# Queries and keys of six latent heads in two parts with three score passes, and three centred tiles instead of four in the second norms

## The reference, cut to what matters

```python
# heads B: 8 heads, query and key of 96 rows (64 from the latent projection, 32 with rotary positions)
s = einsum("bhqd,bhkd->bhqk", q, k) * 96 ** -0.5
p = softmax(s); o = einsum("bhqk,bhkd->bhqd", p, v)
# after the mixer, and again after the feed-forward:
z = ALPHA * x + f(x)
x = (z - mean(z)) * rsqrt(var(z) + eps) * g + b
```

## Time and profile before

| | us |
|---|---|
| median of 3 runs | 2478.61 (2478.15 to 2480.41) |
| the profiled execution, its own time | 2479.52 |
| its span, first to last instruction | 2477.7 |
| PE busy, share of the span | 2409.3, 97% |
| POOL busy | 1895.6, 77% |
| DVE busy | 1168.4, 47% |
| ACT busy | 697.4, 28% |
| mean granted TensorE clock | 0.995 |

### The profile page before, as it was taken

How to read it: one execution, slowest core, us unless ns; L and a number is a source line. 1 busy time by engine, 2 the same in 40 slices (tenths; PEclk the granted TensorE clock), 3 DMA queues, 4 the chain that set the end, 5 groups by cost and what they waited for, 6 DMA issues and landing times.

```text
span 2477.7 us, 32293 instructions
## 1 busy us (share of the span) xinstructions
PE 2409.3 (97%) x11126; PEld 1861.6 (75%) x11126; DVE 1168.4 (47%) x1581; ACT 697.4 (28%) x1262; POOL 1895.6 (77%) x1543
## 2 busy tenths in 40 slices
PE   8999999999999999999999999999999999999998
PEld 6755778888778844788888777767888877678886
DVE  6576443333271477533342485655322656553223
ACT  2266242330021166232220233244010241440101
POOL 8712688889888743898888798836999888369995
PEclk9999999999999999999999999999999999999999
DMA  4201122222223200232222232211222232112222
GB/s 178 85 17 35 60 78 100 93 102 93 94 77 111 85 26 9 70 109 93 95 93 101 77 115 102 85 43 60 94 102 93 94 102 94 39 57 101 93 102 85
DMA packets 57548, 207.12 MB, mean 84 GB/s; under 512 B 6512, under 2 KB 6896, under 8 KB 57200
## 3 DMA queue, kind: packets, MB, share of 16 engines
q1 hardware_dynamic: 55872, 199.87, 23.2%
q10 hardware_dynamic: 1584, 5.96, 0.7%
HBM read 203.71 MB, written 2.10 MB: 83 GB/s over the span
## 4 chain that ended last, share of the span: by engine, by line
PE 85%; DVE 6%; POOL 5%; issue 2%; ACT 1%; DMA 1%; DVEq 0%; POOLq 0%; SPq 0%; ACTq 0%
PE bank L733 23%; PE bank L735 23%; PE bank L734 23%; PE bank L838 3%; PE bank L789 3%; POOL w_hi L2646 2%; POOL w_lo L2649 2%; PE bank L897 2%; PE bank L867 2%; PE bank L918 1%; DMA ring<-in_weights 1%; DVE branch_lo L1934 1%; DVE work L1974 1%; DVE work L1991 1%; PE bank L937 1%
## 5 line engine op out<-in xcount | busy, mean ns | idle before, releaser
L2646 POOL TENSOR_TENSOR w_hi<-ring,unit 128x512 fp32r<-128x512 f32 x734 | 826.6, 1126 | 439.2 <-PE bank L735 300.8
L2649 POOL TENSOR_TENSOR w_lo<-ring,w_hi 128x512 fp32r<-128x512 f32 x734 | 998.2, 1360 | 57.5
L733 PE MATMUL bank<-moving_hi,w_hi 128*128 128x512 f32 x1834 | 723.4, 394 | 21.9 <-DVE moving_lo L2233 9.9
L735 PE MATMUL bank<-moving_hi,w_lo 128*128 128x512 f32 x1834 | 715.8, 390 | 0.0
L734 PE MATMUL bank<-moving_lo,w_hi 128*128 128x512 f32 x1834 | 715.6, 390 | 0.0
L733 PEld LDWEIGHTS bank<-moving_hi,w_hi 128*128 128x128 f32 x1834 | 345.3, 188 | 106.7 <-issue 20.6
L734 PEld LDWEIGHTS bank<-moving_lo,w_hi 128*128 128x128 f32 x1834 | 345.6, 188 | 72.8 <-issue 1.9
L735 PEld LDWEIGHTS bank<-moving_hi,w_lo 128*128 128x128 f32 x1834 | 345.0, 188 | 72.9
L2593 DVE TENSOR_TENSOR region<-region,bank 128x512 f32<-128x512 f32 x64 | 39.7, 681 | 278.4 <-PE bank L735 278.4
L1871 ACT ACTIVATE region<-bank 128x512 f32<-128x512 f32 x64 | 38.1, 598 | 363.5 <-PE bank L735 363.4
L733 PE MATMUL bank<-hid_hi,w_hi 128*128 (+1 forms) x352 | 137.7, 391 | 0.0
(11 more groups left out here) (334 smaller groups left out, 3603.8 us busy)
## 6 DMA issues: line engine op xcount, KB each, us to landing
ring<-in_weights SPq DMA_DIRECT2D x375, 512.0 KB, 3.2
x<-in_x_t ACTq DMA_DIRECT2D x4, 512.0 KB, 8.4
out<-region SPq DMA_DIRECT2D x8, 256.0 KB, 2.2
region<-in_tables ACTq DMA_DIRECT2D x1, 1312.0 KB, 6.2
region<-in_tables ACTq DMA_DIRECT2D x1, 1024.0 KB, 5.7
region<-in_p_t ACTq DMA_DIRECT2D x2, 512.0 KB, 5.3
region<-in_tables SPq DMA_DIRECT2D x1, 320.0 KB, 10.3
small_w<-in_small_w ACTq DMA_DIRECT2D x1, 320.0 KB, 6.0
```

The lines of the kernel that those rows point to most:

```text
L733: pe.matmul(bank, lhs[0], rhs[0], start=start, stop=False, skip_group_check=True)
L735: return pe.matmul(bank, lhs[1], rhs[0], start=False, stop=stop, skip_group_check=True)
L2646: pool.tensor_tensor(w_parts[0][:, s, at], ring[:, s, at], unit[:, 0:1].broadcast_to([P, BLK // 2]), ALU.mult).then_inc(split_hi, 1)
L2649: pool.tensor_tensor(w_parts[1][:, s, at], ring[:, s, at], w_parts[0][:, s, at].bitcast(F32), ALU.subtract).then_inc(split_ready, 1)
```

## The change

Three things. First, POOL makes two fp32r parts of the queries and keys of heads B2 to B7 (units B1 to B3), in a new `split_heads`, called ahead of the split of ("mixout", 0, 0): for each of 3 units, 2 tensors and 2 heads, one multiplication by 1 and one subtraction over 96 partitions x 512, so 24 operations. The lower part is written over the whole tile. `scores` waits for a unit's four splits at its first turn and makes three fp32r passes for each head in place of the one f32 matmul. Unit B0 stays as it was. Secondly, `CENTRED` goes from (1, 4, 1, 4) to (1, 3, 1, 3): in the second norms DVE centres three tiles, POOL five. Thirdly, POOL does four of these (tiles 3 to 6) where it did four before (tiles 4 to 7), and the last one (tile 7) between the two halves of its split of ("plegate", layer, 1).

```diff
-CENTRED = (1, 4, 1, 4)
+CENTRED = (1, 3, 1, 3)
...
+        ab_lower = [nc.alloc_sbuf_tensor_at(f"{name}_b_lo", [P, 8, S], F32R, offset=region_at + 1024 * kb)
+                    for name, kb in (("q", 64), ("k", 92))]
+        ab_upper = [nc.alloc_sbuf_tensor_at(f"upper_b_{n}", [P, S], F32R, offset=region_at + 1024 * kb)
+                    for n, kb in enumerate((88, 90, 108, 110, 112, 114, 116, 118, 120, 122, 124, 126))]
...
-                for c in range(2):
-                    mm = pe.matmul(at[c], q(u, c)[:, i * P:i * P + P], k(u, c)[:, 0:w], start=True, stop=True)
+                if in_parts and in_parts(u, i):
+                    for a, b in ((0, 0), (0, 1), (1, 0)):
+                        for c in range(2):
+                            q_part, k_part = in_parts(u, i)[c]
+                            mm = pe.matmul(at[c], q_part[a][:, i * P:i * P + P], k_part[b][:, 0:w], start=(a + b == 0),
+                                           stop=(a == 1), skip_group_check=True)
+                else:
+                    for c in range(2):
+                        mm = pe.matmul(at[c], q(u, c)[:, i * P:i * P + P], k(u, c)[:, 0:w], start=True, stop=True)
...
+                def parts_b(u, i):
+
+                    j = u[1]
+                    if u[0] == "A" or j == 0:
+                        return None
+                    if i == 0:
+                        pe.wait_ge(heads_split, 4 * j)
+                    rows = slice(0, B_QK)
+                    return [[(ab_upper[4 * (j - 1) + 2 * part + c][rows, :], ab_lower[part][rows, 2 * j + c, :])
+                             for part in range(2)] for c in range(2)]
...
-                early, ahead = (2, 3) if i % 2 else (0, 1)
+                early, ahead = (2, CENTRED[i]) if i % 2 else (0, CENTRED[i])
...
-                    if ahead <= n < CENTRED[i]:
-                        centre(n)
-                        dve.wait_ge(centered, sum(CENTRED[:i]) + n + 1)
...
-            def split(s, n, used=None):
+            def split(s, n, used=None, between=None):
...
+                    if h and between:
+                        between()
...
+            def split_heads():
+
+                pool.wait_ge(roped, ROPE_AT[("qB", 1)] + 1)
+                pool.wait_ge(qb_stored, B_HEADS)
+                rows, n = slice(0, B_QK), 0
+                for j in range(1, B_HEADS // 2):
+                    for part, whole in enumerate((q_b, k_b)):
+                        if j == 1 and part:
+                            pool.wait_ge(kb_stored, B_HEADS)
+                            pool.wait_ge(kpe_spread, B_HEADS // 2)
+                        for c in range(2):
+                            hi, lo = ab_upper[n][rows, :], ab_lower[part][rows, 2 * j + c, :]
+                            tile = whole[rows, 2 * j + c, :]
+                            n += 1
+                            pool.tensor_tensor(hi, tile, unit[rows, 0:1].broadcast_to([B_QK, S]), ALU.mult).then_inc(head_upper, 1)
+                            pool.wait_ge(head_upper, n)
+                            pool.tensor_tensor(lo, tile, hi.bitcast(F32), ALU.subtract).then_inc(heads_split, 1)
...
-            def recentre(i):
+            def recentre(i, last=KD):
...
-                for n in range(CENTRED[i], KD):
+                for n in range(KD - 1 if last is None else CENTRED[i], last or KD):
...
+            def recentre_odd(i):
+
+                recentre(i, KD - 1)
+                n = AT[("plegate", i // 2, 1)]
+                split(n % RING, n, (16 * (n // RING) + 16, n - RING + 1), lambda: recentre(i, None))
+
...
-            for key, between in ((("gate", 0, 0), lambda: recentre(0)), (("pleproj", 0, 0), lambda: recentre(1)),
+            for key, between in ((("mixout", 0, 0), split_heads), (("gate", 0, 0), lambda: recentre(0)), (("pleproj", 0, 0), lambda: recentre_odd(1)),
...
-                ahead = 1 if key[0] == "mixout" else RING
+                ahead = key[1] if key[0] == "mixout" else RING
```

More of the change, by code:

```diff
@@ L582, in build @@
         scored, maxed, exped, scaled = sem("scored"), sem("maxed"), sem("exped"), sem("scaled")
+        head_upper, heads_split = sem("head_upper"), sem("heads_split")
         turned, pt_stored, weighed, attended = sem("turned"), sem("pt_stored"), sem("weighed"), sem("attended")
@@ L828, in tokens_values, with scores @@
                     mm.then_inc(block_done, 1)
-            def scores(u, i, q, k, extra, causal=False):
+            def scores(u, i, q, k, extra, causal=False, in_parts=None):
                 t = TURN_AT[(u, i)]
@@ L845, in heads_in_pairs @@
             def heads_in_pairs(units, q, k, v, extra, causal=False, seed=None, between=None, last_rope=None,
-                               second=None, opened=None):
+                               second=None, opened=None, in_parts=None):
                 turns = [(u, i) for u in units for i in range(ST)]
@@ L879, in heads_in_pairs @@
                         second()
-                    scores(u, i, q, k, extra, causal)
+                    scores(u, i, q, k, extra, causal, in_parts)
                     if last_rope and i == 0:
@@ L889, in heads_in_pairs @@
                     if n + AHEAD < len(turns):
-                        scores(*turns[n + AHEAD], q, k, extra, causal)
+                        scores(*turns[n + AHEAD], q, k, extra, causal, in_parts)
                     t = TURN_AT[(u, i)]
@@ L1180, in last_keys @@
                         pe.wait_ge(roped, ROPE_AT[("qkA", 7)] + 1)
+                def parts_b(u, i):
[7 more added lines that the diff above has]
+                             for part in range(2)] for c in range(2)]
                 heads_in_pairs([u for u in UNITS if u[0] == kind], q, k, v, lambda u: [],
-                               last_rope=("qkA", 6) if kind == "A" else None, opened=opened,
+                               last_rope=("qkA", 6) if kind == "A" else None, opened=opened, in_parts=parts_b,
                                between=last_keys if kind == "A" else None)
@@ L2694, in _ @@
                 split(s, s)
+            def recentre_odd(i):
+                recentre(i, KD - 1)
+                n = AT[("plegate", i // 2, 1)]
+                split(n % RING, n, (16 * (n // RING) + 16, n - RING + 1), lambda: recentre(i, None))
             at = RING
-            for key, between in ((("gate", 0, 0), lambda: recentre(0)), (("pleproj", 0, 0), lambda: recentre(1)),
+            for key, between in ((("mixout", 0, 0), split_heads), (("gate", 0, 0), lambda: recentre(0)), (("pleproj", 0, 0), lambda: recentre_odd(1)),
                                  (("mixout", 1, 0), lambda: scale_first([u for u in UNITS if u[0] == "C"])),
-                                 (("gate", 1, 0), lambda: recentre(2)), (("pleproj", 1, 0), lambda: recentre(3))):
-                ahead = 1 if key[0] == "mixout" else RING
+                                 (("gate", 1, 0), lambda: recentre(2)), (("pleproj", 1, 0), lambda: recentre_odd(3))):
+                ahead = key[1] if key[0] == "mixout" else RING
                 split_up_to(at, AT[key] + ahead)
@@ L2702, in _ @@
                 between()
+                if key[0] == "pleproj":
+                    at += 1
             for layer in range(DEPTH):
```

## The result

| | before | after |
|---|---|---|
| median of 9 runs of each, us | 2479.48 | 2486.37 |
| lowest and highest, us | 2478.15 to 2481.80 | 2483.30 to 2488.84 |
| span of the profiled execution, us | 2477.7 | 2485.0 |

The ratio is 1.0025, with a 95% interval of 1.0017 to 1.0033: the change makes the kernel slower by 4 to 8 us. The forecast was 2487.3 in a range of 2474 to 2492.

A forecast was written before the change was run, and what follows sets the result against it. PE, busy 97% of the span, was taken as the bound, with DVE setting turns 1 to 3 of heads B. Heads +11.7 and norms -3.0 made +8.7 us, from 2478.6 to about 2487.3, range 2474 to 2492.

The forecast's parts named there:

- POOL's work on DVE: Heads B, turns 1 to 3: four DVE operations wait for POOL, 3.7 us a turn; turn 5 13.7 us late.
- that sign: Heads B, changed profile: the chain of waits should go through DVE and POOL from 203 to 237 us.
- The copy beside POOL: Heads B: DVE's copy from SBUF waits 0.97 us for a POOL operation, taken between nothing and 0.97.
- Scores on PE: Heads B: six fp32r matmuls take 1.57 us against 1.82, 0.25 us less a turn, 2.0 over eight turns.
- PE's clock in heads B: Heads B, PE's gaps of about 3 us in three turns: half rate costs nothing, up to 3 us for the range.
- The rival that priced this at up to 3 us: Heads B: PE at 1.2 GHz behind the gaps costs up to 3 us more, 2488 to 2491 us; chance 0.12.
- Norms: Second norms: 1.8 us gained in layer 0 and 1.2 in layer 1, 3.0 together, bounds 1.0 and 4.7.
- The start: Second norms: PE starts the pair of gate blocks 1.95 us earlier, at POOL's split instead of DVE's fourth centring.
- The slow clock behind the gap: Second norms: PE's slow clock behind its 2.5 us gap may go in layer 0; none was seen in layer 1.
- What stayed free: Behind POOL's splits: mixout blocks ready at about 237 us, PE wants them after 262; no cost, 25 us of cover.
- half the waits: Heads B: only the subtraction waits, 3.9 us, about 2477; with some scalings up to 2483 us; chance 0.21.

The follow-up runs named there:

- experiment 2: Two kernels against the one before, norms as before: POOL makes all 24 splits unread, 2494.2 us (+13.6); three passes on ready tiles without splits, 2477.01 us.
- the paced version: Against the change: only units B2 and B3 split, each POOL pair waiting for DVE's scalings, turn 8's pending step at turn 10; with new norms 2474.45 us.

## Why the prediction was right

The forecast was +8.7 us; measured were +6.9 by the medians and +7.3 by the spans. The mechanism was right, and the number is closer than its terms: by the traces the heads cost 1.5 us less than forecast and the norms gave 1.5 more (2.9 + 1.6 against 3.0), which would have made +5.7. The 1.5 us of PE's slow clock in the first norm of layer 1, which nobody forecast, brought the spans back to +7.3. That part is luck.

*POOL's work on DVE.* Right, in place and in kind. The forecast put turn 4's maximum at 225.3, and it came at 225.49. Two errors cancelled on the way. In turn 0 I let the subtraction alone wait, +1.0, but the copy waited too (1.51 us in the trace of after), and turn 1's maximum came 205.60 - 203.66 = 1.9 late, of which 0.1 was there when turn 0 began. Turns 1 to 3 grew by 3.4 to 3.5 us, not 3.7. That term took POOL's pair at the 3.15 us of the earlier trace rows, where every DVE operation has two inputs. Beside turns in which one operation in four has two, the pair takes 2.63, and the four waits average 3.45 / 4 = 0.86. That scalings wait I had read from the earlier trace rows, whose scalings have 384 columns and not 512; at 512 two of them took 2.46 to 2.60 us. The same holds for turns 4 and 5, which I put at 3.9 us; the maxima of turns 4, 5 and 6 stand 3.70 and 3.84 apart (225.49, 229.19, 233.03), and turn 5's transposes came 12.8 late, not 13.7. That is 0.9 of the difference. The chain was to name DVE and POOL; it names DVE alone, and that sign was wrong.

*The copy beside POOL.* No row of before showed one, and I took a whole wait. It took 1.26 to 1.51 us beside POOL in every turn that had it, against 0.42. The Trainium skill, SBUF — State Buffer, section "SBUF: two separate sides", has such a copy and a GpSimd operation exclude each other for a whole instruction; the trace agrees for DVE, whose copies are longer by 0.8 to 1.1 us, up to one POOL operation each. For POOL it shows less: its pair is longer by 0.26 us in the mean, where a DVE copy or scaling lasts 0.4.

*Scores on PE.* The gain was 3.80 - 3.47 = 0.33 us a turn, not 0.25, within the bounds of 0 to 0.44. The six matmuls took 1.49 us of the turn, where the subtraction from eight gave 1.57. Over eight turns that is 2.6 us given back instead of 2.0. Together with the 0.9 above it makes 11.7 - 0.9 - 0.6 = 10.2, which is the trace's figure and that of the timed runs of the heads alone.

*PE's clock in heads B.* It did fall, to a mean of 0.62 over 18 us, and cost nothing that the trace shows, as forecast: DVE had no idle time ahead of the maxima of turns 1 to 4, so PE at half rate still came in time. The rival that priced this at up to 3 us falls.

*Norms.* The direction and the mechanism were right, the size was short: -3.0 forecast, -4.1 and -5.9 in the timed runs of the norms alone, -2.9 and -1.6 in the traces of before and after. Two terms were mis-sized, and both are in the traces. The start: PE starts 0.25 us behind POOL's split (700.54 to 700.79), which my sum held only in part, so it came 1.75 earlier and not 1.95; but where the clock was 1.00 before and after, in layer 1, 1.6 of that lasted, where I took 1.2. The slow clock behind the gap: I gave layer 0 the possibility and layer 1 none, because in the one profile of before the clock fell only in layer 0. In the seven profiled kernels with the old norms it fell behind 12 of the 14 gaps of 2.45 us, in layer 0 in all seven and in layer 1 in five. Layer 1 in the kernel with heads alone, windows as before:

```profile
1424.58:1427.88 3.30, 3.30 (x8) 2.65 (x9) 3.27 (x4) 1.14 (x2) 0.80 (x1) 0.54 0.41 129
```

PE gets through 8 matmuls in 3.3 us there, against 14 in the window of after. Six matmuls of 0.23 us are 1.4 us. In the six profiled kernels with the new norms the clock fell behind none of the 12 gaps of 0.7 us. So the usual gain in layer 1 is the 1.6 of the traces and about 1 more. The stretch behind the second norm of layer 1 took 62.2 to 62.7 us in the five kernels where the clock had fallen, 61.15 in the two where it had not, 59.6 in the six with the new norms. The stretch that holds layer 0's pair took 349.0 to 349.2 us in the seven, 346.2 to 346.3 in the six. With 2.9 in layer 0 that makes 5.5, near the -5.9 and above the -4.1. Here one profile was read as the rule for all executions. That the clock is what makes the difference is read from these traces; no run changes it alone.

*What stayed free.* The two mixout blocks were ready at 235.4, not 237, and PE took them from 272.6 on; nothing waited for them, as the chain shows. The last rival, half the waits, fell with experiment 2, which put POOL's work at +13.6.

What stays open: why PE's slow stretch behind the same gap is short in one profile and long or absent in another, which moves stretches that the change does not touch by up to 1.5 us. The 1.5 us that the paced version may gain over the norms alone is smaller than what these runs tell apart.

## What to carry to other kernels

Idle time of GpSimd is not free cover while VectorE sets the pace with operations from SBUF to SBUF: here each of them waited 0.86 us in the mean, most of a GpSimd operation, and busy time that grows while the work shrinks is the sign of it. Count the operations of that kind in VectorE's turn, and put GpSimd's beside VectorE's reads of PSUM, one pair a turn by a wait, not in a row; here that gave 2.4 us in the trace, but nothing that the timed runs tell from the time before. Where PE's gap is long enough for its clock to fall sometimes, closing it is worth the gap and the slow stretch behind it, and one profile does not tell how often that happens.

## What the runs showed of the hardware

- The interference between the two engines is lopsided: beside each other a scaling and a copy of 512 columns went from about 0.4 us to between 1.2 and 1.5, while POOL's pair went only from 2.37 to 2.63 in the mean. A maximum over 1024 columns of PSUM kept its 1.21 us.
- The clock behind an equal gap in the same code differs from one profile to another: behind 2.45 us of idle PE it fell to a mean of 0.51 to 0.62 over the next 3.3 us in 12 cases and stayed at 1.00 in 2. Behind 0.70 to 0.73 us it stayed in all 12. Behind 4.94 us the lower clock lasted 2.7 us in one profile and 6.1 in another.
- Scores over 96 rows with 512 columns: two float32 matmuls take 1.82 us of PE's turn, six in fp32r 1.49.
